# Splitting each 1024-element dot product over a gathered row into two of 512 elements

## The reference, cut to what matters

```
def peer_ffn(h, w_q, sub_keys, u_tab, v_tab):
    ...                                   # per token and head: 16 indices idx, 16 softmax weights g
        u = u_tab[idx]
        act = jax.nn.gelu(jnp.einsum('thkd,td->thk', u, hb))
        wts = (g * act.astype(jnp.float32)).astype(hb.dtype)
        v = v_tab[idx]
        return jnp.einsum('thk,thkd->td', wts, v)
```

## Time and profile before

| what | value |
|---|---|
| time, median of 3 runs | 2532.51 us (2529.66 to 2547.18) |
| the profiled execution's own time | 2546.51 us |
| its span | 2544.5 us |
| mean granted TensorE clock of the span | 0.917 |
| instructions | 27270 |
| first `u` gather starts / last `v` gather starts | 492.0 / 1252.1 us |

### The profile page before, as it was taken

The page is one execution under the profiler, slowest core; times in us unless marked ns, Lnnn a source line. Parts: engine busy times, 40 slices in busy tenths (PEclk is TensorE's granted clock), DMA queues, the critical chain, the costliest instruction groups (busy, mean ns, idle before and its releaser), DMA issues.

```text
span 2544.5 us, 27270 instructions
## 1 busy us (share of the span) xinstructions
PE 2110.4 (83%) x8874; PEld 1185.0 (47%) x8875; DVE 1007.0 (40%) x2276; ACT 529.7 (21%) x945; POOL 555.5 (22%) x560
## 2 busy tenths in 40 slices
PE   7698798966655766666779987999999999999997
PEld 6566687832222322222367865444444444444443
DVE  5885511465665665665428423111111111111113
ACT  3414410121111111111122402222222222222221
POOL 0000000267776777677400000000000000000000
PEclk9898899988877877878889997999999999999999
DMA  6275253299898999899933242799999999999995
GB/s 281 100 292 204 108 206 117 77 362 380 304 360 334 365 359 375 326 362 344 403 115 133 100 165 99 305 380 429 429 428 429 429 429 429 429 429 429 429 428 231
DMA packets 111250, 784.27 MB, mean 308 GB/s; under 512 B 12993, under 2 KB 13249, under 8 KB 79585
## 3 DMA queue, kind: packets, MB, share of 16 engines
q1 hardware_dynamic: 37472, 515.18, 49.0%
q0 software_dynamic: 73728, 268.47, 28.2%
HBM read 782.55 MB, written 1.05 MB: 308 GB/s over the span
## 4 chain that ended last, share of the span: by engine, by line
PE 49%; issue 7%; DVE 2%; DMA 2%; POOL 1%; ACT 1%; POOLq 0%; another core or an unknown queue 0%; DVEq 0%; ACTq 0%
PE ps L661 41%; PE ps L810 6%; PE ps L1021 1%; DMA ring<-in_peer_v,arena 1%; DMA ring<-in_peer_u,arena 1%; POOL ring L615 1%; ACT arena L1203 1%; POOL ring L623 0%; PE ps L1052 0%; DVE arena L1647 0%; DVE arena L1650 0%; PE ps L1053 0%; DVE arena L1645 0%; PE ps L978 0%; DVE ring L1898 0%
## 5 line engine op out<-in xcount | busy, mean ns | idle before, releaser
L661 PE MATMUL ps<-ring,arena 128*64 128x512 f32 (+2 forms) x3328 | 743.1, 588 | 41.4 <-issue 40.0
L810 PE MATMUL ps<-ring,arena 128*128 128x512 f32 x1024 | 498.5, 645 | 247.0 <-issue 113.8
L661 PE MATMUL ps<-arena,ring 128*128 128x256 f32 x2272 | 521.1, 388 | 28.2 <-DVEq L1652 8.2
L661 PEld LDWEIGHTS ps<-ring,arena 128*64 128x64 f32 (+1 forms) x3328 | 259.7, 139 | 500.7 <-issue 499.4
L661 PEld LDWEIGHTS ps<-arena,ring 128*128 128x128 f32 x2272 | 438.4, 195 | 107.7 <-issue 38.1
L810 PEld LDWEIGHTS ps<-ring,arena 128*128 128x128 f32 x1024 | 209.4, 207 | 533.2 <-issue 528.2
L1630 DVE CUSTOM_DVE_ANT_0 ring<-ring,arena 128x1024 f32<-128x1024 f32 x256 | 312.4, 1226 | 172.7 <-DMA ring<-in_peer_u,arena 145.9
L615 POOL DMA_INDIRECT ring<-in_peer_u,arena x256 | 282.8, 1105 | 105.9 <-issue 80.4
L1871 DVE TENSOR_TENSOR arena<-ps,arena 128x512 f32<-128x512 f32 x66 | 45.7, 692 | 651.9 <-PE ps L1021 651.9
L661 PE MATMUL ps<-arena 128*128 128x128 f32 (+5 forms) x1494 | 232.9, 315 | 82.2 <-ACT arena L1122 20.3
L623 POOL DMA_INDIRECT ring<-in_peer_v,arena x256 | 256.6, 1003 | 102.8 <-issue 75.3
(11 more groups left out here) (292 smaller groups left out, 1073.9 us busy)
## 6 DMA issues: line engine op xcount, KB each, us to landing
ring<-in_w_exp SPq DMA_DIRECT2D x192, 2048.0 KB, 17.1
ring<-in_w_in SPq DMA_DIRECT2D x24, 2048.0 KB, 8.7
ring<-in_w_ada SPq DMA_DIRECT2D x12, 2048.0 KB, 9.4
ring<-in_w_out SPq DMA_DIRECT2D x4, 2048.0 KB, 8.2
ring<-in_w_peer_q SPq DMA_DIRECT2D x4, 2048.0 KB, 7.8
ring<-in_w_br_rnn SPq DMA_DIRECT2D x4, 1280.0 KB, 5.4
ring<-in_w_br_attn SPq DMA_DIRECT2D x2, 2048.0 KB, 8.1
ring<-in_peer_u,arena POOLq DMA_INDIRECT x256
```

What stands on the lines that cost most here:

```text
L661: return pe.matmul(o, l, r, start=start, stop=stop)
L810: return pe.matmul(o, l, r, start=start, stop=False, skip_group_check=True)
```

## The change

A second 16-column tile, `upper_dots`, holds the sums of the upper halves. Each dot product becomes two `tensor_tensor_reduce` of 512 elements; the first is marked on DVE's own semaphore, the second counts `s_dot` as the whole one did. After the 16 of a head one wait on the own semaphore and one `tensor_tensor` add of 128 x 16 are put in, before `s_dots` is signalled. `n_dots = 36` accounts for the 18 more counts of each of two heads.

```
+        upper_dots = carve("P", 2, TOPK)
...
+            n_dots = 2 * (TOPK + 2)
...
-                    own.enter(i, n_best + n_route)
+                    own.enter(i, n_best + n_route + n_dots)
...
-                            dve.tensor_tensor_reduce(u_rows[k % 8], u_rows[k % 8], h2_rows[:, tile, :], 1.0, 0.0,
-                                                     ALU.mult, ALU.add, dots[:, par, k:k + 1]).then_inc(s_dot, 1)
+                            lower, upper = u_rows[k % 8][:, 0:512], u_rows[k % 8][:, 512:D]
+                            own.mark(dve.tensor_tensor_reduce(lower, lower, h2_rows[:, tile, 0:512], 1.0, 0.0, ALU.mult,
+                                                              ALU.add, dots[:, par, k:k + 1]))
+                            dve.tensor_tensor_reduce(upper, upper, h2_rows[:, tile, 512:D], 1.0, 0.0, ALU.mult,
+                                                     ALU.add, upper_dots[:, par, k:k + 1]).then_inc(s_dot, 1)
                         dve.wait_ge(s_dot, i * 32 + TOPK * (g + 1) + 8)
+                        own.settle_apart()
+                        own(tt(dots[:, par, :], dots[:, par, :], upper_dots[:, par, :], ALU.add))
                         dve.sem_inc(s_dots, 1)
```

## The result

| what | before | after |
|---|---|---|
| time, median of 4 runs | 2536.03 us (2529.66 to 2547.18) | 2605.06 us (2593.32 to 2620.22) |
| span of the profiled execution | 2544.5 us | 2597.9 us |
| first `u` gather to last `v` gather starts | 492.0 to 1252.1 us | 491.8 to 1299.8 us |

The changed kernel takes 1.0252 times as long, 95% interval 1.0216 to 1.0288: 69 us more. The forecast was 2525.5, with a range up to 2556. The stage of the gathers grew by 48 us, from 760 to 808, and that is most of the 53 by which the profiled spans differ.

A forecast was written before the change was run, and what follows sets the result against it. POOL's gathers, stretched by DVE dot products on a shared port, were taken to bound the gather stage. Terms -13 (POOL's waits), +3 (tail) and +3 (counts) gave -7 us from 2532.5, so 2525.5 us; range 2493 to 2556.

The forecast's parts named there:

- What bounds the stage: Gather stage, slices 8 to 20: POOL's issuing of gathers, stretched by dot products, limits it; POOL's sum makes 760 us.
- The lock: Port shared by POOL and DVE: a gather waits for the running dot product's end, then takes 0.88 us.
- the halves on DVE: Dot products: a half takes 0.692 us, repeats every 0.61; two take 1.22, the extra mostly hidden by DVE's waits.
- the 2.30 us pace: Head 3, back-to-back dot products: a gather every 2.30 us instead of 1.24; forecast that it cannot arise with halves.
- POOL's waits, -13 us: Gathers held up by dot products: shorter halves cut their stretch from 57.6 to 44.4 us, 13 us less.
- The stretch: Time of the 512 gathers above their short form of 0.937 us: 59.9 us before the change.
- The tail, +3 us: Each head's end: the new wait and add cost 0.5 us, delaying `route` in some passes; 3 us taken.
- Counts on the own semaphore: DVE: 36 more counts an iteration and two more waits a head, slow near the transfer ceiling; 3 us taken.
- slow own waits: Rival: the new wait behind odd heads costs 4.5 us each and delays `route`; 36 us, 2568 us, chance 0.10.
- turning point of 3.1 us: The wait for an odd head from which the rival "slow own waits" decides, 25 / 8 us.
- no overlap: Rival: halves take 0.692 us each, 1.38 a dot product, so POOL waits 37 us more; 2569 us, chance 0.06.
- the transfers take the gain: Rival: what POOL gains it waits for again at the transfers, only the tail left; 2532 to 2538 us, chance 0.16.

The follow-up runs named there:

- e8: The changed kernel again, beside the kernel before on a quick chip: 2470.0 us against 2491.0, ratio 0.991.
- e17: Changed kernel with a 256-column memset on POOL behind each gather, quick chip; two runs of this kernel gave 1.046 and 1.044 of the kernel before.
- e11: Kernel before plus a one-element, uncounted tensor_tensor_reduce after each whole dot product, quick chip: 2494.7 us against 2491.0, ratio 1.002.
- e3: Kernel before with whole dot products, plus only the head-end wait and add (of zeros), quick chip: 2492.5 us against 2492.9, ratio 1.000.
- e14: Changed kernel without marks, head-end wait and add, one half's sum left out, slow chip: 2582.7 us against 2531.7 of the kernel before, 1.020.
- e7: Changed kernel marking only the sixteenth lower half of each head, slow chip: 2595.2 us against 2533.4 of the kernel before, ratio 1.022.
- e15: Changed kernel gathering `v` rows of 512 elements, each used for both matmuls, slow chip: 2587.5 us against 2531.7 of the kernel before, 1.019.
- one counter: Changed kernel with both halves counted on `s_dot`, the add signalling `s_dots`, neither new wait: 0.990 of the kernel before twice (quick), 1.016 (slow).

## Why the prediction was wrong

**What bounds the stage: right.** POOL gives the transfers out. Where nothing else disturbs, the stage follows its pace (e8, e17).

**The lock, and the halves on DVE: right.** The rule read from three gathers holds in the changed kernel: of its 512 gathers 240 start within 0.61 us of a half's start, and 97% of them last, to within 0.05 us, what "wait for its end, then 0.88 us" gives. The halves take 693 and 687 ns (forecast 692), repeat every 0.61 to 0.65 us, and the extra instructions cost 4 us, within the noise, where no slow stretch is (e11). The longest `u` gather fell from 1993 to 1433 ns, and the 2.30 us pace is gone.

**POOL's waits, -13 us: right sign, too small.** The stretch fell by 37 us on the slow chip. On quick chips, where the whole change is -21, e3 and e8 put the stretch at 47.7 and 27.8, 20 us less, and the stage at 697 and 679. Starts move: laying the new durations over the old starts left that out, and I put the value near the low end of bounds that went up to 59.9.

**The tail, +3 us: about right on a quick chip,** where it costs nothing that can be measured (1.000, interval 0.998 to 1.001, which holds 3 us). It wasn't run alone on a slow one.

**"Counts on the own semaphore. ... I take 3 us for all, since most heads' ends show no such wait": the step that failed.** It took the slow stretches of the earlier trace rows for few and given, bounded them at 4.5 us for each odd head, and asked only whether the new wait would fall into one. They were not few: the four waits that it named sum to 23 us, DVE was late by 100 us before, in 13 of 16 heads. And they were not given: DVE is late by 193 us after, up to 9.9 at one add, and more behind even heads (128 us, with `best_keys`) than behind the odd ones that it bounded. POOL's waits for dots and `route`, which I had said should not pass 17.8 and 10.1, are 61.9 and 53.7. The step priced a wait on the fixed rest of the program, and what the change altered was how much of the rest ran slow. It also named the wrong thing: with no count and no wait of its own the loss is still 1.020 (e14).

**The rival "slow own waits", 2568, 0.10:** right in sign and in that `route` comes late and POOL waits for it (53.7 us), past its turning point of 3.1 us at the add in 8 heads, though not in the odd heads alone. It was 37 us short, and its cause doesn't stand: neither the counts (e7) nor the waits (e14) are needed. What was held against it, "it takes transfers near the ceiling", doesn't stand either (e15). The range ended at 2556 because this rival and "no overlap" were left out at the top. "No overlap" did not occur (0.61 us for a half), nor did the transfers take the gain.

**The median of one chip.** Against the kernel before on quick chips, the change does what it says, -21 us, a little under 1%. My trace was of a slow chip, and the spread of its executions couldn't tell me: the kernel before spreads by 18 us on a quick chip (2484 to 2502) as it does there (2530 to 2547). So the gain at the port decided the sign where DVE was never late, with 21 us for the 7 forecast, and not where it was.

**What stays open.** What makes a chip quick or slow for this program, and why shorter DVE operations make more slow stretches where they occur. Three things in the traces narrow it down.

- It is the gather stage. Of the 130 us between the changed kernel's profiles of the result and of e8, 129 lie in it, and over all kernels the span less the stage is 1783 to 1799 us on slow chips and 1785 to 1791 on quick ones.
- The traces of slow chips hold 10,779 to 11,472 semaphore updates, those of quick chips 17,499 to 18,303, of nearly the same program, and the missing ones are all of that stage: 3038 to 3739 are recorded in it against 9750 to 10,572, outside it 7642 to 7762 everywhere. So on a slow chip the time of a wait can be relied on, and less the name of what ended it.
- In the slow stretches the recorded updates come 0.70 to 0.71 us apart (median; after, 619 to 638 us; before, 620 to 643 and 843 to 862), and the distances of the instructions are multiples of that. At the same place of e8 there are 16 in one us.

Whether the missing records and the late instructions have one cause wasn't shown. One rival no kernel here can test: that recording itself holds up the engines there. All timed executions have a recorded span and clock, so nothing tells what either kernel takes without recording. Untested for want of a slow chip: POOL's pace.

**A better version.** On quick chips one counter is the quickest, 0.990 twice, level with the changed kernel within the intervals. On a slow chip it loses 1.016, against 1.023 and 1.025 of the changed kernel elsewhere; they weren't run on one slow chip, and the intervals of 1.016 and 1.023 overlap. No version beat the kernel before on both kinds.

## What to carry over

A gather that shares its port with a long two-input DVE operation gets shorter when that operation is cut in pieces (here 0.991 where the engines ran undisturbed). Before pricing an added instruction, look in the trace for stretches in which an engine's instructions follow each other at fixed distances longer than they last: there an instruction can cost several times its duration, and a trace of before doesn't bound it. A change worth 1% should be compared beside the kernel before on more than one chip, since its sign can differ between them.

## What was unexpected of the hardware

- The same kernel takes 2486 to 2493 us on three chips and 2532 to 2536 on at least two others, and outside the gather stage no profile shows a difference of that size. The granted clock over the stage, 0.84 in e8 and 0.78 to 0.82 in the slow profiles, doesn't set them apart: in e17, on a quick chip and with DVE never late, it is 0.79 over a stage of 808 us.
- In slow stretches instructions of DVE and TensorE come 1.4 and 2.8 us apart, and small operations of 0.2 us wait up to 10 us. Recorded semaphore updates come 0.7 us apart there.
- There 512 short DVE instructions cost 27 us (0.05 us each), on a quick chip 4 us, within the noise.
- Gathers get in between two DVE operations that follow back to back, 0.88 us from the first one's end to the gather's, and the second doesn't wait for them visibly: halves kept their 0.61 to 0.65 us.
